# One low half of weights per expert on GpSimd, with the expert's output rows scaled ahead of it on VectorE

## What is computed

```python
h = modulate(rmsnorm(x, norm2_g[l]), sh2, sc2)
x = x + g2[:, None, :] * moe(h, ...)
# moe: route() picks 2 of 16 experts for each row, with weights that sum to 1
# each expert: y = (silu(xb @ w_gate[e]) * (xb @ w_up[e])) @ w_down[e]   (1024 -> 512 -> 1024)
# the rows of y are weighted and summed back to their token
```

## Time and profile before

| | us |
|---|---|
| median of 3 runs | 1479.87 |
| lowest and highest of them | 1477.39, 1480.16 |
| the profiled execution | 1479.38 |
| its span in the profile | 1477.8 |
| busy: TensorE matmuls | 1442.4 |
| busy: VectorE | 1133.3 |
| busy: ScalarE | 773.2 |
| busy: GpSimd | 143.4 |

### The profile page before, as it was taken

The page is one execution under the profiler, slowest core; times in us unless marked ns, Lnnn a source line. Parts: engine busy times, 40 slices in busy tenths (PEclk is TensorE's granted clock), DMA queues, the critical chain, the costliest instruction groups (busy, mean ns, idle before and its releaser), DMA issues.

```text
span 1477.8 us, 18814 instructions
## 1 busy us (share of the span) xinstructions
PE 1442.4 (98%) x6824; PEld 1155.0 (78%) x6824; DVE 1133.3 (77%) x1532; ACT 773.2 (52%) x1102; POOL 143.4 (10%) x139
## 2 busy tenths in 40 slices
PE   6999999999999999999989999999999999999997
PEld 3788887778877778888858888878888787888884
DVE  5774677455669999999987657854345899999998
ACT  3333433223256888888733344342233488888883
POOL 0000001000002211111100000100000112211010
PEclk9999999999999999999999999999999999999999
DMA  8856466455557999999956543642254879999995
GB/s 346 306 185 195 160 212 199 144 186 159 199 205 249 381 390 390 383 392 378 358 220 206 189 140 115 195 145 88 86 171 147 287 283 393 394 388 393 378 378 207
DMA packets 107413, 377.49 MB, mean 255 GB/s; under 512 B 16521, under 2 KB 16713, under 8 KB 106548
## 3 DMA queue, kind: packets, MB, share of 16 engines
q1 hardware_dynamic: 90864, 331.39, 62.0%
q0 software_dynamic: 15200, 40.62, 7.7%
q10 hardware_dynamic: 1252, 4.22, 0.8%
HBM read 361.32 MB, written 34.64 MB: 268 GB/s over the span
## 4 chain that ended last, share of the span: by engine, by line
PE 83%; DVE 11%; DMA 2%; ACT 1%; issue 1%; DVEq 1%; ACTq 0%; SPq 0%
PE ps L1759 25%; PE ps L1761 24%; PE ps L1760 24%; DVE w_lo L1510 3%; DVE w_lo_more L1510 3%; DMA raw<-w 2%; PE ps L1844 2%; PE ps L2018 1%; PE ps L1913 1%; PE ps L2067 1%; PE ps L1917 1%; DVE xgT_lo L1499 1%; DVE y_out L1533 1%; DVE w_lo L1007 1%; PE ps L1948 0%
## 5 line engine op out<-in xcount | busy, mean ns | idle before, releaser
L1007 DVE TENSOR_TENSOR w_lo<-raw,w_hi 128x1024 fp32r<-128x1024 f32 x132 | 161.3, 1224 | 213.9 <-ACT w_hi L651 212.6
L651 ACT ACTIVATE w_hi<-raw 128x1024 fp32r<-128x1024 f32 x132 | 139.1, 1058 | 334.2 <-PE ps L1761 332.5
L1510 DVE TENSOR_TENSOR w_lo<-raw,w_hi 128x1024 fp32r<-128x1024 f32 x188 | 224.2, 1216 | 3.9 <-ACT w_hi L836 3.0
L1759 PE MATMUL ps<-w_hi,hT_lo 128*128 128x512 f32 x512 | 206.6, 404 | 4.1 <-DVE hT_lo L1110 4.1
L1510 DVE TENSOR_TENSOR w_lo_more<-raw,w_hi_more 128x1024 fp32r<-128x1024 f32 x172 | 205.2, 1216 | 2.4 <-ACT w_hi_more L836 1.3
L836 ACT ACTIVATE w_hi<-raw 128x1024 fp32r<-128x1024 f32 x188 | 193.5, 1058 | 24.5 <-DMA raw<-w 15.1
L1761 PE MATMUL ps<-w_hi,hT_hi 128*128 128x512 f32 x512 | 200.4, 391 | 0.0
L1760 PE MATMUL ps<-w_lo,hT_hi 128*128 128x512 f32 x512 | 200.0, 391 | 0.0
L836 ACT ACTIVATE w_hi_more<-raw 128x1024 fp32r<-128x1024 f32 x172 | 177.0, 1057 | 25.2 <-DMA raw<-w 15.7
L1759 PE MATMUL ps<-hT_hi,w_lo 128*128 128x512 f32 x320 | 130.5, 408 | 0.0
L1761 PE MATMUL ps<-hT_hi,w_hi 128*128 128x512 f32 x320 | 125.0, 391 | 0.0
(11 more groups left out here) (285 smaller groups left out, 2629.1 us busy)
## 6 DMA issues: line engine op xcount, KB each, us to landing
raw<-w SPq DMA_DIRECT2D x590, 512.0 KB, 7.2
h_rows<-h POOLq DMA_DIRECT2D x8, 1024.0 KB, 5.2
ahead<-w SPq DMA_DIRECT2D x4, 2048.0 KB, 11.2
x_state<-x POOLq DMA_DIRECT2D x2, 2048.0 KB, 10.1
y_rows<-x_in ACTq DMA_DIRECT2D x4, 1024.0 KB, 12.5
x<-x_state POOLq DMA_DIRECT2D x4, 1024.0 KB, 6.1
pair_early<-y_rows SPq DMA_DIRECT2D x4, 1024.0 KB, 6.4
x<-x_in SPq DMA_DIRECT2D x4, 512.0 KB, 12.8
```

The lines of the kernel that those rows point to most:

```text
L651: act.activation(w_hi[:, q % W_SLOTS], stream_piece(l, q, r), ACT.Copy).then_inc(w_hi_ready, 1)
L1007: v.tensor_tensor(w_lo[:, q % W_SLOTS], stream_piece(l, q, r), w_hi[:, q % W_SLOTS], ALU.subtract).then_inc(raw_used, 1)
L1510: v.tensor_tensor(ring_lo(e * EXP + n), expert_piece(e, n), ring_hi(e * EXP + n), ALU.subtract).then_inc(raw_used, 1)
L1759: pe.matmul(dst, a_lo, b_hi, start=start, stop=False)
```

## The change

In the experts 1 to 14 of both layers VectorE leaves the first low half of its batch to GpSimd. VectorE begins the batch with `rows_out(e - 1)`, waits for GpSimd's semaphore `pool_lo`, makes the second low half, and adds 2 to `raw_used` with it, for both pieces. GpSimd does the subtraction for expert e + 1 in its part of expert e, between the gather and the wait for `y_copied`, as soon as ScalarE has made the high half. Expert 0 and expert 15 keep their order.

```diff
+        pool_lo = sem("pool_lo")
...
-                def lo_e(n):
+                def lo_e(n, pieces_done=1):
                     v.wait_ge(w_hi_ready, q0 + (MIX + n + 1))
                     v.tensor_tensor(ring_lo(e * EXP + n), expert_piece(e, n), ring_hi(e * EXP + n),
-                                    ALU.subtract).then_inc(raw_used, 1)
+                                    ALU.subtract).then_inc(raw_used, pieces_done)
...
                 else:
-                    lo_e(next(pieces))
-                    lo_e(next(pieces))
                     if e:
+                        next(pieces)
                         rows_out(e - 1)
+                        v.wait_ge(pool_lo, l * (NE - 2) + e)
+                        lo_e(next(pieces), 2)
+                    else:
+                        lo_e(next(pieces))
+                        lo_e(next(pieces))
                     hidden(0)
...
                 if e == NE - 1:
                     return
+                if e + 1 < NE - 1:
+                    n = LEAD[e + 1]
+                    r = (e + 1) * EXP + n
+                    pool.wait_ge(w_hi_ready, l * PROD + (MIX + r + 1))
+                    pool.tensor_tensor(ring_lo(r), expert_piece(e + 1, n), ring_hi(r), ALU.subtract).then_inc(pool_lo, 1)
                 pool.wait_ge(y_copied, E + 2)
```

## The result

| | before | after |
|---|---|---|
| median (lowest, highest) of 4 runs each, us | 1479.05 (1477.39, 1480.16) | 1489.53 (1489.02, 1489.78) |
| the profiled execution, its span | 1479.38, 1477.8 | 1489.73, 1488.1 |

The ratio of after to before is 1.0076, 95% interval 1.0065 to 1.0088. The forecast of 1479.4 and its range up to 1488 were both missed, on the slow side.

A forecast was written before the change was run, and what follows sets the result against it. TensorE was taken to set the pace, VectorE to bound experts 2 to 4 of each layer, with DMA as near. 1479.38 + 0.14 - 0.1 = 1479.4 us; range 1474 to 1488.

The forecast's parts named there:

- x: Time from ScalarE's end of the high half to VectorE's start on the next low half: 2.5 us, range 1.2 to 3.5.
- rival B: VectorE and GpSimd block each other's SBUF reads: +1.2 us in up to eight experts, 1489; chance 0.08.
- Rival C: GpSimd's handover takes 4 us or more; TensorE loses once per layer: 1482.6 at 4, 1484.6 at 5; chance 0.07.
- the late experts: Experts at TensorE's pace: `hid` moves by +0.07 us, each layer ends that much later, +0.14 in all.
- the early experts: Experts 2 to 4 of each layer, bound by VectorE: `hid` gains 0.55 us once, counted as -0.1 for all.
- Rival A: Landings not at their limit, early experts go from 18.41 to 17.65 us: 1473.3, half of it 1476.4; chance 0.22.
- Slots: Both pieces released together, so SyncE's loads go out up to 2.5 us later; DMA queue stays filled: zero cost.
- Rival D: Late pair of releases thins the DMA queue: 0.3 us per expert, 8.4 in all, 1487.8; chance 0.07.

The follow-up runs named there:

- The first-expert run: The change kept in expert 1 of both layers alone, other experts as in the kernel before: 1481.55 us beside 1478.25, ratio 1.0025.
- the kernel without the hold: The changed kernel, but GpSimd starts its subtraction only when VectorE has done the low half before it: 1490.97 us beside 1477.93, ratio 1.0083.
- the copy: The kernel before plus an unused 128x1024 copy on GpSimd (one operand read) in experts 2 to 14: 1484.28 us, one execution.
- the fill: The kernel before plus an unused 128x1024 zero fill on GpSimd (nothing read) in experts 2 to 14: 1478.92 us, one execution.
- the extra subtraction: The kernel before plus an unused 128x1024 subtraction on GpSimd in experts 2 to 14: 1493.2 us beside 1477.93, ratio 1.0108.

## Why the prediction was wrong, step by step

**Right in most late experts: x.** Forecast 2.5 us from ScalarE's end to VectorE's next low half. The high half for expert 6 ended at 569.94 (568.88 + 1.06), and:

```profile
570.03 2.40 POOL L2277 TENSOR_TENSOR w_lo<-raw,w_hi 128x1024 fp32r<-128x1024 f32 x1 [11.66 <-ACT w_hi L837]
```

```profile
569.84 1.22 DVE L1534 TENSOR_TENSOR y_out<-ps,gate_row 128x1024 f32<-128x1024 f32 x1
572.51 1.23 DVE L1511 TENSOR_TENSOR w_lo<-raw,w_hi 128x1024 fp32r<-128x1024 f32 x1 [1.46 <-POOL w_lo L2277]
```

The subtraction took 2.40 us where I had 2.3, the handovers 0.09 and 0.08, and x is 2.57. VectorE waits 1.46 us, forecast 1.3. In twelve of the twenty late experts x is 2.57 to 2.66: GpSimd starts beside `y_out` or in the last 0.2 us of a low half. In the other eight x is 2.76 to 3.33: GpSimd starts earlier in a low half of VectorE and takes 2.58 to 3.15 us. Such a case in expert 13 of layer 0, where the second of two low halves ends at 694.57:

```profile
693.75 3.08 POOL L2277 TENSOR_TENSOR w_lo_more<-raw,w_hi_more 128x1024 fp32r<-128x1024 f32 x1 [12.40 <-ACT w_hi_more L837]
...
692.22 2.35 DVE L1511 TENSOR_TENSOR w_lo<-raw,w_hi 128x1024 fp32r<-128x1024 f32 x2
```

That is the hold of rival B with the parts exchanged. The Trainium skill (GPSIMD Engine Reference, Performance versus the Vector engine), from which I had estimated 2.25, came within 7% of the 2.40. Rival C, x of 4 us and more, is out for late experts.

**Right as far as can be told: the late experts.** +0.07 per layer was forecast, and the twenty late experts alone gave no difference that can be told from zero. A difference of 0.14 us is too small for these runs, so they confirm that the loss is small and not how it was worked out.

**Right that little was to be gained: the early experts.** I counted -0.1, and leaving the work out altogether gave only -1.6, with landings as 27% of the chain. Rival A, 3 to 6 us faster, did not come: of its periods at TensorE's own pace only one in each layer appeared, and that in the kernel without the work. In the change itself ScalarE's waits for landings became shorter, where I had said that they would grow.

**The step that failed: "Slots".** It reads: "SyncE's loads for these slots, and those queued behind them, go out up to 2.5 us later ... no cost", and ends with "I count zero". I had asked who waits for `raw_used` and answered: SyncE. But TensorE waits for it too, "before it uses the piece", as the description of the kernel says further up. And where I asked who stands behind the waiting VectorE, I named the next low half and `hid`, "for which TensorE's transposes wait", and not the piece of that low half. In late experts both omissions are harmless: with `LEAD` at 8 the piece is used half an expert later. With `LEAD` at 4 TensorE wants piece 1-4 at 474.32, 2.9 us after ScalarE has made its high half (471.40). In the kernel before, the first low half of this pair ended at 474.29:

```profile
473.07 2.35 DVE L1510 TENSOR_TENSOR w_lo<-raw,w_hi 128x1024 fp32r<-128x1024 f32 x2
```

How soon TensorE comes for it, the kernel that only releases later tells: there the pair starts at 471.13, so its first low half ends at 472.35, and TensorE wants the piece at 473.25, 0.9 us after. A release 2.5 us later could not fit in there. The cost: 1.9 us per layer in expert 1 (some 1.25 from telling late, 0.65 from the slower piece), and of the 2.2 in expert 2 the 0.9 that go when the piece is told of at once, 0.61 of them as the wait for 2-5. The first-expert run shows the former (+3.3 in all, 2 x 1.9 by the periods), the run that releases at once the latter.

**Underrated and misplaced: rival B.** It said that GpSimd's read makes a low half stand still for 2.3 us, decides from a lead of ScalarE of one low half on, and costs 1.2 in each of eight experts: 1489, with a chance of 0.08. The mechanism is real: in after exactly four low halves take 3.42 us, two in each layer, 2.2 us longer than the others, and with them the busy time that the page misses. The place is not as told: it happens in batches 1 and 2 only; in batch 3 ScalarE waits for a landing again, its high half ends at 532.40, and the subtraction meets only the rest of VectorE's last low half and then `y_out`. It costs TensorE 1.35 us per layer for piece 2-4, and most of the +0.7 behind it, where `hid` comes 0.93 us late (+0.1 in the kernel without the hold): together about 2, some 4 in both layers, and by the kernels without the hold, whose GpSimd starts later, at least 1.2 to 1.4, some 2.6 in both. That B's 1489 is the time measured is a coincidence: less than half of the loss is B's. The Trainium skill (SBUF — State Buffer, Who interferes with whom) states just this hold, and that a GpSimd instruction that only writes is free of it; the copy and the fill agree. I gave that rule no term in the sum but only a chance of 0.08, and noted that no row of before shows both engines at such work at once. No row could: GpSimd computes nothing of this kind there. That is no evidence against it.

**Rival D, "the late pair of releases lets the DMA queue run thin",** is not excluded as a small part. Its own sign, a share under 0.95 in late experts, is absent (the windows of the experts 5 to 13 have 0.98 to 1.02), the late experts of the change cost at most 2.4 us, and ScalarE waits less for landings in the early ones than before. But the late release alone gave +3 us in late experts, and in the windows of expert 1 and 2 after the DMA share is 0.89 and 0.95; released at once it is 0.95 and 1.00 again, like the 0.97 and 1.02 of before. Whether the thinner queue costs anything of its own there, or only follows TensorE's waits, no run tells.

**The sum, as the runs give it:** late release and slow piece in expert 1, 2 x 1.9; in expert 2, 2 x 2.2, in which TensorE's wait for the held piece is 1.35 each; expert 3, 2 x 0.7; expert 4, -0.4 and +0.2; the rest of the layers 0.9 + 0.6. From the unrounded periods that is 11.1, less 0.7 ahead of and between the layers, against 10.3 between the two spans. The terms of the later experts, 1.5 in all, are within what one execution differs from another. One slip of the prediction, without weight: its times for other x (1481.5, 1482.6, 1484.6) count the 0.14 twice.

## What to carry to other kernels

When a semaphore's increment is moved or joined with a later one, list every engine that waits on it, and for each of them how soon after the increment it comes, expert by expert (stage by stage), where the lead is smallest and not where it is usual. Work moved to GpSimd beside a busy VectorE costs VectorE time wherever both read SBUF at once; put it where VectorE reads PSUM or waits anyway, and count the hold as a term of the sum. And ask first what the relief is worth by leaving the work out: here 1.6 us, and that with the pair released together.

## What the runs showed of the hardware

- A subtraction of 128x1024 fp32 takes GpSimd 2.40 us (2.39 to 2.41 in the kernel where it starts behind VectorE's low half), VectorE 1.22 (1.135 from start to start). A copy of that size takes GpSimd 1.17 us, a fill 0.96.
- While GpSimd reads SBUF, a low half of VectorE can stand still (3.42 us in after, 2.92 and 2.06 beside the extra subtraction and copy, none beside the fill); VectorE's `y_out`, which has one operand in PSUM, does not: 1.22 us at 569.84, with the subtraction beside it from 570.03.
- What I had not expected: the hold goes both ways. In sixteen of the 26 extra subtractions GpSimd is the one that waits: 4.8 to 5.8 us instead of 2.51, while VectorE loses little (0.23 us on a low half that follows). In the change itself GpSimd's subtraction takes up to 3.15 us where it starts beside a running low half, 2.40 where it starts beside `y_out`; whoever waits for its result waits with it.
